# Attention inside a fused two-layer decoder: products with the values one query block later, query blocks in another order

## The reference, cut to what matters

```
q_full = concat(q_nope, rope(q_pe)) * 96 ** -0.5          # 8 heads, 96 wide
k_full = concat(k_nope, rope(k_pe) shared by the heads)   # 96 wide
for each block of 128 queries:
    sc  = q_full[block] @ k_full.T ; masked where key > query
    out = softmax(sc) @ v                                 # v: 64 wide a head
```

## Time and profile before

| | |
|---|---|
| median of 3 runs | 2352.89 us (2352.69 to 2354.26) |
| the profiled execution | 2351.72 us |
| its span | 2349.9 us |
| granted TensorE clock, mean over the span | 0.991 |
| PE busy over the span | 2276.1 us, 97% |
| DVE, ACT, POOL busy | 57%, 38%, 44% |

### The profile page before, as it was taken

One profiled execution on the slowest core, in us unless ns is written; L12 is line 12 of the kernel. 1 busy time (PEld: TensorE's weight loads), 2 busy tenths in 40 slices (PEclk: granted clock), 3 DMA queues, 4 the chain that ended last, 5 costly groups with the idle time before them and its releaser, 6 DMA issues.

```text
span 2349.9 us, 31829 instructions
## 1 busy us (share of the span) xinstructions
PE 2276.1 (97%) x10415; PEld 1850.8 (79%) x10415; DVE 1337.8 (57%) x2177; ACT 903.8 (38%) x1595; POOL 1034.3 (44%) x715
## 2 busy tenths in 40 slices
PE   6998999999999999999989999999999999999998
PEld 5786777778888888888868878878788888888886
DVE  7756565248755555555671115663875555555556
ACT  4535555124433333333441114451433333333333
POOL 3413333333555555555433332214335555555554
PEclk9999999999999999999999999999999999999998
DMA  4100000311111111111231110012111111111112
GB/s 167 45 27 1 1 0 28 117 36 45 37 54 53 47 52 46 52 54 54 64 124 55 45 45 28 27 56 92 34 36 54 54 53 47 52 46 52 54 54 90
DMA packets 34583, 122.07 MB, mean 52 GB/s; under 512 B 3840, under 2 KB 3968, under 8 KB 34240
## 3 DMA queue, kind: packets, MB, share of 16 engines
q1 hardware_dynamic: 31328, 105.39, 14.3%
q10 hardware_dynamic: 3168, 15.54, 1.7%
HBM read 112.52 MB, written 8.39 MB: 51 GB/s over the span
## 4 chain that ended last, share of the span: by engine, by line
PE 89%; DVE 7%; ACT 2%; issue 2%; POOL 0%; DMA 0%; ACTq 0%; DVEq 0%; POOLq 0%
PE ps L808 10%; PE ps L806 10%; PE ps L810 10%; PE ps L728 9%; PE ps L730 9%; PE ps L729 9%; PE ps L846 6%; PE ps L848 6%; PE ps L847 6%; PE ps L1571 2%; PE ps L1718 1%; PE ps L1722 1%; PE ps L1720 1%; PE ps L1559 1%; PE ps L603 1%
## 5 line engine op out<-in xcount | busy, mean ns | idle before, releaser
L509 POOL TENSOR_TENSOR wlo<-stage,whi 128x512 fp32r<-128x512 f32 x308 | 397.3, 1295 | 459.4 <-ACT whi L971 455.5
L728 PE MATMUL ps<-ahi,whi 128*128 128x512 f32 x896 | 368.8, 412 | 29.8 <-POOL wlo L434 19.1
L427 POOL TENSOR_TENSOR whi<-stage,cons 128x1024 fp32r<-128x1024 f32 x64 | 125.5, 1962 | 527.8 <-PE ps L730 313.4
L730 PE MATMUL ps<-ahi,wlo 128*128 128x512 f32 x896 | 351.2, 392 | 0.0
L729 PE MATMUL ps<-alo,whi 128*128 128x512 f32 x896 | 351.0, 392 | 0.0
L971 ACT CAST whi<-stage 128x512 fp32r<-128x512 f32 x308 | 189.2, 620 | 363.5 <-POOL stage L522 181.0
L1231 DVE TENSOR_TENSOR hT<-hT,ps 128x512 f32<-128x512 f32 x352 | 238.9, 686 | 153.9 <-PE ps L848 153.8
L846 PE MATMUL ps<-hid_hi,whi 128*128 128x512 f32 x640 | 251.3, 393 | 1.8 <-DVE hT L1231 1.6
L848 PE MATMUL ps<-hid_hi,wlo 128*128 128x512 f32 x640 | 249.8, 390 | 0.0
L847 PE MATMUL ps<-hid_lo,whi 128*128 128x512 f32 x640 | 249.6, 390 | 0.0
L806 PE MATMUL ps<-ahi,whi 128*128 128x512 f32 x608 | 236.7, 389 | 0.0
(11 more groups left out here) (323 smaller groups left out, 4089.6 us busy)
## 6 DMA issues: line engine op xcount, KB each, us to landing
stage<-in_wt SPq DMA_DIRECT2D x184, 512.0 KB, 3.6
hT<-in_xt SPq DMA_DIRECT2D x16, 256.0 KB, 9.6
hT<-in_xt ACTq DMA_DIRECT2D x8, 512.0 KB, 8.3
spill<-hT ACTq DMA_DIRECT2D x1, 4096.0 KB, 12.1
hT<-spill ACTq DMA_DIRECT2D x8, 512.0 KB, 8.2
out<-hT SPq DMA_DIRECT2D x16, 256.0 KB, 2.1
wqb_s<-in_wqb ACTq DMA_DIRECT2D x1, 1024.0 KB, 4.8
wlru_s<-in_wlru ACTq DMA_DIRECT2D x1, 512.0 KB, 6.4
```

The lines of the kernel that those rows point to most:

```text
L509: nc.gpsimd.tensor_tensor(block_lo(c), src, block_hi(c).bitcast(F32), ALU.subtract).then_inc(sem(L + "b_ready"), 1)
L728: nc.tensor.matmul(bank, hi, rhs_k[0][:, tok], start=k_first, stop=False)
L730: return nc.tensor.matmul(bank, lo, rhs_k[0][:, tok], start=False, stop=k_last)
```

## The change

The list `order` becomes 7 0 6 1 5 2 4 3 (sizes 8 1 7 2 6 3 5 4). In PE's step i, `weigh` now works on step i-1; step 0 of a pair has none and step 15 has two, for steps 14 and 15. DVE's `outputs` moves in the same way. The semaphore counts that `scores` waits for at the beginning of a head are adapted: both first steps of a head now wait for `qk_lo`, since block 0 needs the first half of the queries. ACT's and POOL's programs keep their order of calls, and only the sizes of the steps change in them.

```diff
-        order = [6, 7, 0, 1, 4, 5, 2, 3]
+        order = [7, 0, 6, 1, 5, 2, 4, 3]
...
-                if k in (0, 2):
-                    pe.wait_ge(sem("qk_lo"), h * 4 + (3 if isinstance(step, int) and step < 2 else 4))
+                if k < 2:
+                    pe.wait_ge(sem("qk_lo"), h * 4 + (3 if isinstance(step, int) and step == 0 else 4))
...
-                    weigh(p * 2 + par, k, step, grp)
+                    for before in ([i - 1] if i >= 1 else []) + ([i] if i == 15 else []):
+                        was, kb = before // 8, before % 8
+                        weigh(p * 2 + was, kb, p * 16 + before, p * 24 + (12 * was + groups_before[kb]))
...
-                    outputs(p, par, k, p * 16 + i)
+                    for before in ([i - 1] if i >= 1 else []) + ([i] if i == 15 else []):
+                        outputs(p, before // 8, before % 8, p * 16 + before)
```

## The result

| | before | after |
|---|---|---|
| median (5 runs each) | 2352.82 us (2352.56 to 2354.26) | 2375.75 us (2374.88 to 2376.42) |
| ratio, 95% interval | | 1.0094 (1.0084 to 1.0105) |
| span of the profiled execution | 2349.9 us | 2373.1 us |
| mean granted clock | 0.991 | 0.985 |

The account below looks back on a forecast made before the run. PE, busy for 97% of the span, was taken to bound the kernel. Added 24.4 us less removed 17.4 made it 7.0 us slower, 2359.9 against the median, forecast 2360 us; 8-in-10 range 2347 to 2368.

Parts of the forecast that it names:

- (a): `weigh` waits 19 times for ACT's copy of the turned probabilities; the delay removes this, 13.8 us (bounds 10.8 and 13.8).
- (b): At the start of pairs 1 to 3 the first projection's 0.84 us wait for `y_lo` is hidden: 2.5 us removed.
- (c): Key projection for k = 2 stands 0.16 us behind the rotation; more transposes ahead cover it, seven times: 1.1 us removed.
- (d): Second query projection waits for bank 0 to empty, 2.44 us in first heads, 1.49 in second: 12.6 us added.
- (e): Products of sizes 5 and 6 wait for DVE's scaling, queued behind maxima of later blocks: 5.6 and 1.5 us added.
- (f): Step 15's second product waits 0.6 us until `outputs` has read the first from bank 7, four times: 2.4 us added.
- (g): Last head, without projections: products wait further behind the maxima, 0.6, 0.9 and 0.3 us: 1.8 us added.
- (h): Stage opens with size 8, so scores, maximum and exponentials before the first transpose take longer: 0.5 us added.
- rival 3: Clock falls after longer PE stands: 1.35 us behind each of seven second-projection waits, 9.5 us in all, 2369 us; chance 0.10.
- Rivals 1: DVE keeps up, so the waits behind its scaling are covered: no change, 2353 us; chance 0.20.
- 2: Bank 0 is free as early as now relative to PE, second projection's added wait nothing: 2347 us; chance 0.14.

Follow-up runs that it names:

- run 1: Changed kernel with unused matmuls filling PE's stands, but for the first and those of the last head: 2362.51 us, ratio 1.0038.
- run 4: Kernel before, last operation of the first rotation done four times, lengthening the second projection's wait from 0.25 to 2.4 us in seven heads: 2382.3 us.
- run 3: Changed kernel with unused matmuls only at the ends of heads and seams, none before the projection: 2367.47 us, ratio 1.0051.
- run 7: Kernel before with only the delay: products with the values one step later, old order of blocks: 2359.91 us, ratio 1.0021.
- run 9: Kernel before with products delayed one step and, for k 0 and 1, put before the projection; old order of blocks: 2374.89 us, ratio 1.0083.
- run 10: Kernel before with products delayed one step, old order, projections at k 0, 2, 3, 4 in place of 0, 1, 2, 3: 2360.92 us, ratio 1.0029.

## Why the prediction was wrong

The steps of the sum, in us, with what the changed kernel shows (each wait of a list has 0.16 us added, as in the prediction):

| step | forecast | measured |
|---|---|---|
| (a) `weigh` for its copy | -13.8 | -13.8, gone from PE's list |
| (b), (c) first and third projection | -3.6 | -2.2, see below |
| (d) second projection | +12.6 | 14.0 + 7 x 0.16 less 7 x 0.24: +13.4 |
| (e), (f), (g) products behind the scaling | +11.3 | 9.0 + 17 x 0.16: +11.7 |
| (h) the start | +0.5 | 210.52 - 204.62 against 210.20 - 204.94: +0.6 |
| sum of the waits | +7.0 | +9.7 |
| clock inside the stage | 0 | +12.4, the rest of 22.1 |
| outside the stage | 0 | +1.1 |

**The waits were right,** each to about 1.5 us, with their places: 2.53 and 1.68 us at the second projection where 2.44 and 1.49 were reckoned, 0.85 at the products of size 5 where 0.8 was, 0.67 for the second product of step 15 where 0.6 was. Step (b) was counted on three seams from the rows of one. The first projections of the three, in the kernel before (the first is in the earlier trace rows):

```profile
320.69 0.47 PE L1515 MATMUL ps<-lat_hi,wh_hi 128*128 128x512 f32 x1 [0.65 <-DVE alo L2396]
...
375.41 0.59 PE L1515 MATMUL ps<-lat_hi,wh_hi 128*128 128x512 f32 x1
```

The third seam had no such wait to remove, since PE, at half clock there, came as late as the data: 1.6 us went and not 2.5. Of (c), the gap before the third projection fell from 0.16 to 0.08 us seven times: 0.6 and not 1.1.

**The step that failed** is the clock, which the sum put at nothing: the prediction left it to rival 3 with "I give it little" and a chance of 0.10, because the same stand had brought a fall at 372 us and none at 264. The runs showed 12.4 us in its place. Pieces at half clock account for 11.7 of them. Three seams lose 2.8 each (7.0 less 4.2) and three second heads 1.6 each (4.79 less 3.19). The start loses 1.0 more than before (210.52 to 215.95 less 3.5 us of pieces, against 0.85), and before lost 1.3 at 372 us and 1.2 from 421 us to the end of the stage that after does not. 0.7 us stay unplaced. Runs 1 and 4 show the cause: the same stands with PE kept busy cost 12.5 us less, and the same wait put into the kernel before costs twice its length.

Rival 3 as written expected the falls behind the seven new waits, at 1.35 us each. In the changed kernel four of these seven, the longest (2.5 us, in first heads), have none: 280.32 runs at full speed, after the half clock of the seam has ended. Three have one, and the three seams have one, where the stands are 0.85, 0.67 and 0.69 us in a row. So the total of rival 3 (2369) came nearer than the forecast, but with partly wrong places and sizes: its seven falls of 1.35 us stand against six of 1.6 and 2.8.

What I drew from the earlier trace rows, two equal stands and one fall, was that falls are rare. The runs fit the other reading, that the kernel stood close to where its clock falls. They do not show what decides where it falls: neither the length of the stand (2.5 us brought none here and two falls in run 3) nor the sum of the waits does (runs 7 and 9, and run 10 against the kernel before). That stays open. (PE's longest stand before was also not 0.8 us, as rival 3 had it, but 1.0 in the list, some 1.2 with the 0.16 added.)

**Rivals 1 and 2** fell: DVE did not keep up (17 waits for the scaling), and bank 0 was not free earlier. That DVE had idle time (it is busy for 124.67 of 242 us) was no argument, as stated.

**Outside the stage** nothing of the program differs. The first scores start 0.3 us earlier, and behind the stage 1.4 us are lost. The changed kernel was granted a clock of 0.83 in two stretches of 10 us (530 and 1220 us) where before had 1.00 (1.7 us each), and before lost 1.4 us to a clock of 0.76 in 424 to 430 us, where after has 1.00. Other runs show such stretches in other places; they were not tested.

## What to carry to other kernels

A wait on a nearly full TensorE can cost twice its length when the stretch around it already has stands: 15.1 us of waits cost 29 here, 9.7 cost 22.1. With PE kept busy through most of them, the second set cost 9.5 (run 1). So look in the old trace for places where the clock has fallen once, and give the fall a term of its own in the sum; unused matmuls in the stands tell afterwards how much of a loss is clock. Before moving work out from between two uses of a single buffer, add up the buffer's whole chain over all its uses: filling one gap moves the wait to the next. A delayed consumer also needs its own consumer's place in the next engine's queue checked, since it lands behind later and larger work there.

## What the runs showed that I had not expected

- PE with useless matmuls in its stands finished the stage 12.5 us earlier (229.0 against 241.5).
- The fall is not set by the longest stand: 2.53 us brought none and 1.68 us one, in each of three pairs. Filling only the projection's stands also took away one of three falls at seams, and filling only the others took away two of three in second heads and brought two in first heads.
- Sums of waiting within 1.1 us of each other gave stages 15.6 us apart (runs 7 and 9: 228.1 and 243.6, clocks 0.95 and 0.90), and within 0.4 us 7.8 apart (run 10 and the kernel before).
- The new order alone costs as much as order and delay together (2376.36 and 2375.75), the delay alone 5 us (2.6 to 7.3). None of the twelve was faster than the kernel before.
